# A two-layer decoder trunk on one core: the residual is kept with tokens on partitions, and gates, branches, output and down projections move 512 weight columns at a time

## The reference, cut to what matters

```python
D_MODEL = 1024; SEQ = 256; DEPTH = 2; BRANCH_WIDTH = 512; D_FF = 2816; N_EXPERTS = 8; D_EXPERT = 1408; TOP_K = 2
def rms_norm(x, g):
    y = x * lax.rsqrt(jnp.mean(x * x, axis=-1, keepdims=True) + EPS)
    return y * g
def reference(x, ...):
    for layer in range(DEPTH):
        h = rms_norm(x, g_mix[layer])
        proj = h @ w_in[layer]                       # 1024 x 5936
        (c_q, c_kv, k_rope, gla_q, gla_k, gla_v, gla_lr, gla_og, u_pool, gate_logits) = jnp.split(proj, split_points, axis=-1)
        y_a = mla_branch(...)                        # 8 heads, causal softmax attention
        y_b = gla_branch(...)                        # gated linear attention; ends rms_norm(o, g_out) * silu(out_gate)
        y_c = pool_branch(...)
        y_d = jnp.einsum('bsnc,ncd->bsnd', jnp.stack([y_a, y_b, y_c], axis=2), w_branch[layer])   # 3 x (512 x 1024)
        gates = jax.nn.sigmoid(gate_logits.reshape(B, S, 3, D_MODEL))
        x = x + jnp.sum(gates * y_d, axis=2) @ w_out[layer]
        h = rms_norm(x, g_ffn[layer])
        if layer % 2 == 0: x = x + swiglu(h, w_ffn_gate[0], w_ffn_up[0], w_ffn_down[0])           # 2816 wide
        else:              x = x + moe_ffn(h, w_router, w_e_gate, w_e_up, w_e_down)               # 8 experts, top 2
    return x
```

## Time and profile before

| | |
|---|---|
| median of 3 runs | 1288.3 us |
| the profiled execution | 1289.96 us, its span 1288.2 us |
| PE busy | 93% of the span |
| DVE / ACT / POOL busy | 66% / 54% / 7% |
| mean granted TensorE clock | 0.964 of full speed |
| DMA | 248 MB, 193 GB/s on average, 294 GB/s in the expert stage |

### The profile page before, as it was taken

The page is one execution under the profiler, slowest core; times in us unless marked ns, Lnnn a source line. Parts: engine busy times, 40 slices in busy tenths (PEclk is TensorE's granted clock), DMA queues, the critical chain, the costliest instruction groups (busy, mean ns, idle before and its releaser), DMA issues.

```text
span 1288.2 us, 21002 instructions
## 1 busy us (share of the span) xinstructions
PE 1202.6 (93%) x8365; PEld 1099.4 (85%) x8365; DVE 845.7 (66%) x1090; ACT 700.3 (54%) x937; POOL 88.7 (7%) x148
## 2 busy tenths in 40 slices
PE   5999799988999998999889998799999999999996
PEld 4988788987999998979879898788888888888885
DVE  4456776585545544523686587488888888888884
ACT  4654454645434434554355455376766666666663
POOL 5001412000000000000252100000000000000000
PEclk8998999999999999997899999799999999999998
DMA  6442243436536543342334445289889898988981
GB/s 196 132 151 79 74 142 124 162 104 240 181 134 226 180 148 122 107 131 66 106 98 132 134 165 191 84 292 340 299 307 321 288 338 289 341 306 291 333 286 61
DMA packets 162660, 248.07 MB, mean 193 GB/s; under 512 B 4254, under 2 KB 140564, under 8 KB 162580
## 3 DMA queue, kind: packets, MB, share of 16 engines
q1 hardware_dynamic: 161328, 246.82, 56.6%
q10 hardware_dynamic: 1252, 0.13, 0.1%
HBM read 245.89 MB, written 1.05 MB: 192 GB/s over the span
## 4 chain that ended last, share of the span: by engine, by line
PE 80%; DVE 10%; ACT 4%; issue 4%; POOL 2%; POOLq 0%; ACTq 0%; DVEq 0%
PE PS L526 24%; PE PS L928 9%; PE PS L930 9%; PE PS L929 9%; PE PS L811 5%; PE PS L812 5%; PE PS L813 5%; DVE m_lo L1565 3%; PE PS L887 2%; PE PS L490 2%; DVE w_lo L326 2%; ACT w_hi L318 2%; PE PS L623 2%; PE PS L899 1%; DVE small L1693 1%
## 5 line engine op out<-in xcount | busy, mean ns | idle before, releaser
L326 DVE TENSOR_TENSOR w_lo<-ring,w_hi 128x1536 fp32r<-128x1536 f32 (+1 forms) x240 | 388.0, 1623 | 153.1 <-ACT w_hi L318 151.8
L318 ACT ACTIVATE w_hi<-ring 128x1536 fp32r<-128x1536 f32 (+1 forms) x240 | 329.1, 1378 | 159.8 <-PE PS L813 86.0
L1565 DVE TENSOR_TENSOR m_lo<-ring,m_hi 128x512 fp32r<-128x512 f32 (+2 forms) x256 | 188.1, 763 | 125.8 <-ACT m_hi L1160 124.9
L1160 ACT ACTIVATE m_hi<-ring 128x512 fp32r<-128x512 f32 (+2 forms) x256 | 157.4, 629 | 161.1 <-PE PS L526 160.7
L526 PE MATMUL PS<-h_hi,m_hi 128*128 128x256 f32 (+2 forms) x672 | 201.2, 299 | 15.2 <-issue 7.4
L526 PE MATMUL PS<-h_lo,m_hi 128*128 128x256 f32 (+2 forms) x672 | 195.1, 290 | 0.0
L526 PE MATMUL PS<-h_hi,m_lo 128*128 128x256 f32 (+2 forms) x672 | 194.8, 290 | 0.0
L928 PE MATMUL PS<-w_hi,hTe_hi 128*96 128x384 f32 (+1 forms) x512 | 168.5, 329 | 6.9 <-DVE w_lo L326 5.7
L929 PE MATMUL PS<-w_hi,hTe_lo 128*96 128x384 f32 (+1 forms) x512 | 165.1, 323 | 0.0
L930 PE MATMUL PS<-w_lo,hTe_hi 128*96 128x384 f32 (+1 forms) x512 | 165.1, 322 | 0.0
L526 PEld LDWEIGHTS PS<-h_hi,m_hi 128*128 128x128 f32 (+2 forms) x672 | 132.2, 197 | 20.3 <-issue 17.4
(11 more groups left out here) (301 smaller groups left out, 2197.6 us busy)
## 6 DMA issues: line engine op xcount, KB each, us to landing
ring<-in_w_in_dram SPq DMA_DIRECT2D x40, 1024.0 KB, 5.0
ring<-in_w_exp_gate_dram SPq DMA_DIRECT2D x24, 1536.0 KB, 7.8
ring<-in_w_exp_up_dram SPq DMA_DIRECT2D x24, 1536.0 KB, 8.2
ring<-in_w_exp_down_dram SPq DMA_DIRECT2D x24, 1536.0 KB, 7.1
ring<-in_w_branch_dram SPq DMA_DIRECT2D x12, 1024.0 KB, 5.1
ring<-in_w_ffn_gate_dram SPq DMA_DIRECT2D x6, 1536.0 KB, 7.1
ring<-in_w_ffn_up_dram SPq DMA_DIRECT2D x6, 1536.0 KB, 6.5
ring<-in_w_ffn_down_dram SPq DMA_DIRECT2D x6, 1536.0 KB, 6.3
```

Source lines behind the costliest of these rows:

```text
L318: act.activation(w_hi[:, b, 0:words], ring[:, i % NSLOT, w0:w0 + words], ACT.Copy)\
L326: dve.tensor_tensor(w_lo[:, b, 0:words], ring[:, (j // 2) % NSLOT, w0:w0 + words], w_hi[:, b, 0:words].bitcast(F32), SUB).then_inc(sem(f"l ...
L1160: act.activation(hi, raw, ACT.Copy).then_inc(sem("m_hi_ready"), 1)
L1565: dve.tensor_tensor(lo, raw, hi.bitcast(F32), SUB).then_inc(sem("m_lo_ready"), 1)
```

## The change

The residual becomes `x_tok`, with 128 tokens on partitions and the 1024 channels along the free axis (two token tiles `a`). `x` is loaded straight into it and `y` stored straight from it.

- **Norm** (four times: `hm` and `hf` of both layers). For each token tile ACT takes the row sum of squares, Ln and Exp; DVE scales by the row's factor and the gain row (broadcast to all partitions by a DMA) into `xn`; PE transposes 4 x 128 columns into a bank; ACT and DVE split the bank into `h_hi`, `h_lo`.
- **Matmuls.** Gates, branches, output projection and the dense down projection have the activation stationary (128 x 128) and 512 weight columns moving. A gate load is now 512 columns by half of the depth, two loads make one result, which lies in banks 6 and 7; `go` has moved to the rotation. The merged result is turned by 16 transposes ahead of the output projection.
- **Order.** The first loads are `va vb cq`, `oga`/`ogb` and the turned queries (`rq`) come earlier; `y_b` stands ahead of the merges of the first branch. PE's loop over experts 1 to 6 is unrolled. The output is stored before the number of passes is read.

The core of the diff (left out: the renamed tiles, the list of semaphore counts, the same edit on further lines):

```diff
-            + ["g0", "s0", "s1", "g1", ... "g10", "g11", "ssg0", "ssg1"]
-            + [f"b{n}{m}" for n in (0, 2, 1) for m in range(4)] + [f"w{m}" for m in range(4)] + ["ssf"])
+            + [f"v{v}c{c}" for v in range(2, LEVELS + 1) for c in range(2)] + ["go0", "go1", "ssg0", "ssg1"]
+            + [f"b{n}{hf}{a}" for n in (0, 2) for hf in range(2) for a in range(2)]
+            + ["b100", "b101", "b110", "b111", "mt00", "mt01", "w00", "w01", "mt10", "mt11", "w10", "w11",
+               "hf00", "hf01", "hf10", "hf11"])
...
# PE: a norm's transposes, and the first load of a mixer
+            def turn_h(L, which, a):
+                for c in range(2):
+                    bank, full = begin(L, f"{which}{a}{c}")
+                    pe.wait_ge(sem("xn_ready"), 4 * w + 2 * a + c + 1)
+                    for i in range(4):
+                        mm = pe.transpose(bank[:, i * P:(i + 1) * P], xn[:, a, (4 * c + i) * P:(4 * c + i + 1) * P], ident[:, :])
+                    mm.then_inc(full, 1)
...
             def mixer(L):
-                sumsq(L, "ssm", L)
                 if L == 0:
                     parameters()
+                turn_h(L, "hm", 0)
+                bank, full = begin(L, "va")
+                token_after_token(L, "va", ..., first=lambda a: turn_h(L, "hm", 1) if a else None)
...
                 def gate(i):
-                    pair(L, f"g{i}")
+                    groups = []
+                    for a in range(TT):
+                        if i % 2 == 0 and gate_no(L, i):
+                            pe.wait_ge(sem(f"gate_free{a}"), gate_no(L, i))
+                        groups.append((sem(f"gate_full{a}"), [(PS[:, 6 + a, :], 0, 512, a)]))
+                    by_pieces(L, f"g{i}", groups, k0=i % 2 * 4)
...
-                        pe.matmul(go(h, 0, P), keys, attn[:, c, d * T:d * T + P], start=(h % 2 == 0), stop=False,
+                        bank, full = begin(L, f"go{d}")
...
+                branch(1, 0)
+                branch(1, 1, lambda: turn_merged(0))
+                w0 = [begin(L, f"w0{a}") for a in range(TT)]
+                evacuated(L, "mt00"), evacuated(L, "mt01")
+                out_part(0, w0)
+                turn_merged(1)
...
# PE: dense down projection
-                            mm = three(PS[:, 4 + m // 2, (m % 2) * T:(m % 2 + 1) * T], hi[:, c], lo[:, c],
-                                       hid_hi[:, g0 + t, :], hid_lo[:, g0 + t, :], False, False)
+                                mm = three(PS[:, 4 + 2 * a + c, :], hid_hi[:, g0 + t, tok], hid_lo[:, g0 + t, tok],
+                                           hi[:, w], lo[:, w], False, False)
...
# PE: scatter of an expert's rows, and the loop over experts
-                        mm = pe.matmul(PS[:, 4 + c % 2, j * T:(j + 1) * T], ye[:, kt * P:(kt + 1) * P], selT[:, e, :],
+                    pe.matmul(PS[:, 4 + c % 2, :], selT[:, e, a * P:(a + 1) * P], ye[:, d * 512:(d + 1) * 512],
-                with pe.Fori(1, NE - 1) as e:
+                for e in range(1, NE - 1):
...
# ACT: a norm
+                def inverse(a):
+                    act.activation(squares, x_tok[:, a, :], ACT.Square, accum_out=ssn[:, a:a + 1])
+                    act.activation(rn[:, a:a + 1], ssn[:, a:a + 1], ACT.Ln, bias=eps[:, 0:1], scale=1.0 / D)
+                    act.activation(rn[:, a:a + 1], rn[:, a:a + 1], ACT.Exp, scale=-0.5).then_inc(sem("rn_ready"), 1)
...
+                inverse(0), high(0, 0), inverse(1), high(0, 1), high(1, 0), high(1, 1)
...
# ACT: inverse roots for y_b
                 split(L, "br01")
                 for i in range(2):
-                    inverse_rms(L, 2 + i, f"ssg{i}", 2, 1.0 / GDV, [0])
+                    inverse_rms(L, 1 + i, f"ssg{i}", 2, 1.0 / GDV, [0])
+                for i in range(2):
+                    inverse_rms(L, 1 + i, f"ssg{i}", 2, 1.0 / GDV, [1])
                 split(L, "br20")
-                for i in range(2):
-                    inverse_rms(L, 2 + i, f"ssg{i}", 2, 1.0 / GDV, [1])
...
# DVE: a norm
+                add(0), scaled(0, 0), add(1), scaled(0, 1), low(0, 0), low(0, 1)
+                scaled(1, 0), scaled(1, 1), low(1, 0), low(1, 1)
...
# DVE: y_b
-                split(L, "br01"), merge(0, 0), merge(0, 1)
+                split(L, "br01"), y_b(0), y_b(1), merge(0, 0), merge(0, 1)
                 split(L, "br20"), merge(0, 2), merge(0, 3)
-                split(L, "br21", FIRST), y_b(0), y_b(1), split(L, "br21", LAST)
+                split(L, "br21")
...
# SP: the end
+            store(1)
+            sp.wait_ge(sem("stored"), 64)
             sp.wait_ge(sem("passes_known"), 1)
             npass = sp.value_load(npi[0:1, 0:1], min_val=1, max_val=PASSES)
```

More of the change, by code:

```diff
@@ L637, in mixer @@
                 pe.matmul(bank[0:QK, 0:T], R[NOPE:QK, :], krope[NOPE:QK, :], start=True, stop=True).then_inc(full, 1)
-                pair(L, "ogb")
+                for i in range(4):
+                    bank, full = begin(L, f"rq{i}")
+                    evacuated(L, f"q{i}")
+                    pe.matmul(bank[0:QK, :], R[:, :], q[:, 2 * i:2 * i + 2, :], start=True, stop=True).then_inc(full, 1)
+                pair(L, "ua")
                 pe.wait_ge(sem("rk_ready"), L + 1)
@@ L1236, in mixer @@
                 split(L, "ogb", LAST)
+                for i in range(4):
+                    bank, free = full(L, f"k{i}")
+                    act.activation(sk[0:NOPE, 2 * i:2 * i + 2, :], two(bank[0:NOPE, :]), ACT.Square)
+                    act.activation(k[0:NOPE, 2 * i:2 * i + 2, :], two(bank[0:NOPE, :]), ACT.Copy,
+                                   scale=pcol("g_qk_k", L, NOPE)).then_inc(free, 1)
+                split(L, "ua", FIRST)
+                out_gate(1)
+                split(L, "ua", LAST)
                 bank, free = full(L, "ssq")
```

617 lines of the change are left out of this document (324 added, 293 removed), and 4 rows, old and new, of the table MIX_USES.

## The result

The changed kernel takes 1321.2 us (median of 4 runs, 1315.92 to 1321.71) against 1287.8: a ratio of 1.0248, 95% interval 1.0219 to 1.0276. Run again beside the kernel before (experiment 7) it stood at 1.0214 (1.0176 to 1.0253). So it is slower, by some 30 us (28 to 33), where +22.6 was forecast; 1321.2 lies inside the range of 1298 to 1325.

The account below looks back on a forecast made before the run. The prediction took PE's pace, plus the places where PE stands still, as the bound. Its terms summed to +22.6 us on the profiled 1289.96: 1312.6 profiled, 1311 for the median, with a range of 1298 to 1325.

Parts of the forecast that it names:

- The wait at `br01`: First branch of each mixer: PE idles 7.5 us for banks `y_b` frees, 9.0 with half-clock restart, +18.0 in all.
- The norm ahead of the dense stage: Norm before the dense feed-forward: longer chain on ACT and DVE, +6.9, plus +0.9 for zeroing matmuls.
- The start: First norm of mixer 0: first `va` matmul about 28.1, tile 1's about 37.9, +10.2 us.
- The dense stage's -2.1: Dense down projection: 264 pairs of matmuls become wide ones, saving 0.0078 us each.
- Rival C: Wide matmuls run at their floor of 0.2133 us, saving 35 us; total 1286, chance 0.08.
- rival D: Gates: each pair waits 1.3 us for the last sigmoid reading banks 6 and 7, +13; 1324, chance 0.17 shared.
- rival E: Norms: eight more table loads cost 1.4 us more each, 11 us; total 1322, chance 0.17 shared.
- The scatter (term 5): Experts: 8 fp32 matmuls of 512 columns replace 16 of 256, saving 0.34 us per expert, -2.7 in all.
- The unrolled loop (term 5): Experts: unrolling PE's loop gives -1.0 us, between -5 and 0.
- The router (term 3): Norm ahead of the router: logits copied some 7.4 us later, less 0.3 for rows needing no turning back, +7.1.
- The end (term 6): End of kernel: the store follows the last add, program ends about 1283, -5 us, between -10 and 0.
- The width (term 1): Gates, branches, output, dense down projection: 1320 pairs become 512-column matmuls, 0.0078 us saved each, -10.3.

Follow-up runs that it names:

- experiment 7: The changed kernel measured and profiled once more without an edit: 1316.9 us, 1.0214 of the kernel before.
- experiment 1: Changed kernel with the banks of `go` and the sums of squares swapped and ACT's two Ln ahead of `br01`'s splits: 1306.4 us, 1.0114.
- experiment 2: Changed kernel with Sqrt on ACT and a reciprocal on DVE instead of Ln and Exp in the four norms: 1302.0 us, 1.0078.
- experiment 4: Changed kernel with every 512-column matmul of gates, branches, output, dense down projection and scatter made as two of 256: 1334.2 us, 1.0326.
- Experiment 10: Improved changed kernel (early first norm included), with DVE's low parts of `g0` put ahead of two operations awaiting ACT's exponential: 1261.4 us, 0.9779 of the kernel before.

## Why the prediction was right, and where it was off

**Right.** The sign, and the largest term. The wait at `br01` was 7.58 us in each mixer (7.5 forecast), its chain as written, and experiment 1 took it away; with the restart it was 9.5 (9.0). The norm ahead of the dense stage became 8.3 and 7.3 us longer (7.8). The start was a first matmul of `va` at 28.06 (28.1) and one of tile 1 at 37.95 (37.9). The dense stage's -2.1 was -2.2 and -1.7. Rival C would have needed less than 0.215 us a matmul and found 0.2267; rival D's wait for a sigmoid at the gates does not show among the waits of 0.6 us and more; rival E fell by experiment 2.

The number is less good than that. 1321.2 lies outside of the forecast's own 1304 to 1319 and next to the 1322 to 1324 of rivals D and E, of which neither was there: only the wide range, drawn to take them in, holds it. (The second measurement, 1.0214, would be 1315 on the same base, inside of the forecast's own range.) And misses of either sign are summed in it: the end gave back 2.6 us more than forecast, without which the difference would have been larger still.

**Off, term by term.** The rest, 31.8 - 22.6 = 9.2 us in the first profile and 3.6 in the second, comes from five places in the main.

- *The scatter (term 5), -2.7, was 0.* The step that failed: I took "8 in 1.89 us" as their cost. That is busy time, with the last matmul's tail, which lies under the next. The starts say otherwise, in the kernel before and in the changed one:

```profile
949.00 1.89 PE L899 MATMUL PS<-qk,big 96*128 x8
950.54 0.52 PE L928 MATMUL PS<-w_hi,hTe_hi 128*96 128x384 f32 x1
950.91 0.34 PE L929 MATMUL PS<-w_hi,hTe_lo 128*96 128x384 f32 x1
```

```profile
932.04 1.88 PE L984 MATMUL PS<-big,qk 96*128 96x512 f32 x4
933.36 0.74 PE L1012 MATMUL PS<-w_hi,hTe_hi 128*96 128x384 f32 x1
933.94 0.34 PE L1013 MATMUL PS<-w_hi,hTe_lo 128*96 128x384 f32 x1
```

  From the first fp32 matmul to the second one of the expert's own that follow are 1.91 us (949.00 to 950.91) and 1.90 (932.04 to 933.94). The experts as a whole are 439.4 against 438.8, and experiment 4 finds no cost in halving.
- *The unrolled loop (term 5), -1.0, was 0.* The waits at an expert's start are 0.79 to 1.00 us and still released by `w_lo`, where they were 0.77 before; the term had no row behind it.
- *The router (term 3), +7.1, was +9.7 and +10.0.* Nearly all of the excess lies ahead of the copy of the logits. The router's 32 tiny matmuls, before and changed, took 1.45 us longer, for which the forecast has nothing:

```profile
810.73 5.52 PE L858 MATMUL PS<-wr,big 128*128 128x8 f32 x32 [2.90 <-DVE big L1554]
```

```profile
848.13 6.97 PE L952 MATMUL PS<-wr,hT 128*128 128x8 f32 x32 [1.22 <-issue]
```

  Another 0.8 is a later start of the first addition, 2.46 us behind the output's last matmul instead of 1.62. The windows over the stage, before and changed, show the clock:

```profile
803.60:831.00 27.40, 19.47 (x102) 18.61 (x102) 14.58 (x46) 7.55 (x13) 0.00 (x0) 0.75 0.32 120
```

```profile
833.40:869.70 36.30, 19.32 (x90) 17.88 (x90) 14.95 (x43) 9.41 (x16) 0.00 (x0) 0.58 0.23 86
```

  PE is busy as long with 12 matmuls fewer, at a granted clock of 0.58 instead of 0.75, behind a norm in which it stood still for longer. I had priced the restart at `br01` and nowhere else.
- *The end (term 6), -5, was -7.6.* I had expected some 8 us behind the last add and left PE's 5.7 us of issue in them; it was 5.0.
- *The stages up to the branches.* 1.3 to 1.4 us each are a wait that the forecast does not name: 3.69 us ahead of `g0` became 4.99 and 5.08. Experiment 10 shows that it is DVE's order. In mixer 0 that leaves 2.1 us in the first profile and 0.2 in the second. Of the difference between the two, 1.6 us lie between the starts of two loads in the middle of the mixer (99.96 and 123.95; 99.62 and 121.99), where the granted clock was 0.72 and 0.77; and the 4.3 us between the two in mixer 1 go with a clock of 0.92 and 0.95 (experiment 7).

The width (term 1) was, if anything, under-sized, -10.3 for what experiment 4 puts at 10 to 14: the step was to take the experts' 0.2322 with 96-column stationary operands as the pace of the 128-column ones, which is 0.2267.

**Open.** Why the clock is granted less in one execution than in the next, on the same instructions, no run here tells. Whether the 18 to 22 us of experiment 2 are more than its forecast of 14 stays open too (14.2 against the second profile); what a shorter halt of PE gives by letting the clock come back sooner was not measured by itself.

## What to carry to other kernels

When a result moves from banks that nobody waits for into a rotation, look at who frees it and what that engine still has ahead of it: here the place of `go` in the rotation and of one line on ACT cost 13 to 17 us. On ACT, count the changes of table in the order in which the functions stand for each tile; taking both tiles' Ln before both Exp gave 10 to 14 us, a Sqrt with a reciprocal on DVE 18 to 22. And a gain may be hidden under waits of the same change: undo them one by one before the idea is given up. Here 1.0248 became 0.9894 that way, and 0.9779 with two more orders, of which one was tried on the kernel before as well. And take a second profile of the same kernel before a few us in one stage are read as an edit's effect.
